# Two sets of edits to a hybrid mLSTM and expert-choice kernel: the barrier and the selection rounds between scan and experts; the order of first weights, small products and states

## The reference

```python
hn = rms_norm(x, norm1_g)
gb, gc, u, q, k, v, o, gates = split(hn @ w_in)          # 1024 x 3088
conv_out = gb * short_conv(gc * u, conv_w)
ht = mlstm_scan(q, k, v, li_f, lf_f) + flip(mlstm_scan(flip(q), ...))   # chunks of 128, both directions
mix = concat([conv_out, sigmoid(o) * head_norm(ht)])
x = x + mix @ w_out
tokens = rms_norm(x, norm2_g)
affinity = softmax(tokens @ w_router)                    # 16 experts
gate, idx = top_k(affinity.T, cap)                       # cap: 32 (prompt), 128 (sample)
ye = (silu(xe @ w_gate) * (xe @ w_up)) @ w_down * gate   # per expert, xe = tokens[idx]
y = rms_norm(x + scatter_add(ye, idx), final_g)
```

## Time and profile before

| what | us |
|---|---|
| median of 3 runs | 1314.3 |
| lowest and highest | 1312.56 and 1315.32 |
| profiled execution, its own time | 1317.02 |
| its span | 1315.3 |
| TensorE busy | 1259.4 |
| VectorE busy | 912.3 |
| ScalarE busy | 736.8 |
| GpSimd busy | 322.2 |

### The profile page before, as it was taken

The page is one execution under the profiler, slowest core; times in us unless marked ns, Lnnn a source line. Parts: engine busy times, 40 slices in busy tenths (PEclk is TensorE's granted clock), DMA queues, the critical chain, the costliest instruction groups (busy, mean ns, idle before and its releaser), DMA issues.

```text
span 1315.3 us, 25185 instructions
## 1 busy us (share of the span) xinstructions
PE 1259.4 (96%) x9826; PEld 1032.6 (79%) x9826; DVE 912.3 (69%) x1313; ACT 736.8 (56%) x1066; POOL 322.2 (25%) x316
## 2 busy tenths in 40 slices
PE   7999999999999999759999999999999999999993
PEld 6868987666587888659888988898889888988892
DVE  5463122442577555898889888988898889888975
ACT  6655322123334554346667666766676667666763
POOL 2511321010133331132232313131313131313040
PEclk8999999999999999979999999999999999999997
DMA  8131455251278774269999999999999999999895
GB/s 266 65 117 53 140 166 153 93 165 25 86 236 240 214 211 134 93 225 330 313 303 316 340 315 300 317 337 314 299 316 338 315 301 315 337 316 299 300 365 205
DMA packets 242032, 314.76 MB, mean 239 GB/s; under 512 B 16097, under 2 KB 206049, under 8 KB 241969
## 3 DMA queue, kind: packets, MB, share of 16 engines
q1 hardware_dynamic: 226576, 268.54, 62.1%
q0 software_dynamic: 15392, 45.36, 11.7%
HBM read 274.41 MB, written 39.44 MB: 239 GB/s over the span
## 4 chain that ended last, share of the span: by engine, by line
PE 89%; DVE 4%; ACT 2%; DMA 2%; issue 1%; SPq 0%; POOL 0%; DVEq 0%; ACTq 0%; POOLq 0%
PE psum L2182 22%; PE psum L2048 16%; PE psum L2189 11%; PE psum L2205 8%; PE psum L2030 8%; PE psum L1921 8%; PE psum L2223 4%; PE psum L2214 4%; PE psum L2175 1%; PE psum L1976 1%; DMA woraw<-in_w_out_dram 1%; ACT yt L1203 1%; PE psum L1902 1%; PE psum L1940 1%; PE psum L1981 1%
## 5 line engine op out<-in xcount | busy, mean ns | idle before, releaser
L1769 DVE TENSOR_TENSOR elo<-eraw,ehi 128x2048 bf16<-128x2048 f32 x192 | 433.4, 2284 | 1.0 <-POOLq L815 1.0
L1173 ACT ACTIVATE ehi<-eraw 128x2048 fp32r<-128x2048 f32 x192 | 362.3, 1903 | 26.5 <-PE psum L2223 18.6
L2182 PE MATMUL psum<-xc,ehi 128*128 128x320 f32 x2048 | 330.3, 313 | 2.1 <-DVE xc L1774 2.1
L2182 PEld LDWEIGHTS psum<-xc,ehi 128*128 128x128 f32 x2048 | 302.3, 188 | 3.6 <-DVE xc L1774 2.4
L2189 PE MATMUL psum<-xb,elo 128*128 128x160 bf16 x2048 | 163.9, 233 | 0.0
L1782 DVE TENSOR_REDUCE gu<-psum 128x320 f32<-128x640 f32 x128 | 105.2, 822 | 82.6 <-PE psum L2189 82.3
L2189 PEld LDWEIGHTS psum<-xb,elo 128*128 128x128 bf16 x2048 | 138.5, 98 | 13.1
L2048 PE MATMUL psum<-hn_nar,wnar 128*128 128x512 bf16 (+1 forms) x768 | 144.0, 344 | 0.0
L2205 PE MATMUL psum<-ehi,hc 128*128 128x512 f32 x512 | 132.6, 406 | 0.0
L2048 PEld LDWEIGHTS psum<-hn_nar,wnar 128*128 128x128 bf16 x768 | 72.9, 98 | 63.6 <-issue 4.9
L2205 PEld LDWEIGHTS psum<-ehi,hc 128*128 128x128 f32 x512 | 95.1, 188 | 22.2
(11 more groups left out here) (275 smaller groups left out, 1656.0 us busy)
## 6 DMA issues: line engine op xcount, KB each, us to landing
eraw<-in_w_gate_dram SPq DMA_DIRECT2D x64, 1024.0 KB, 8.9
eraw<-in_w_up_dram SPq DMA_DIRECT2D x64, 1024.0 KB, 8.8
eraw<-in_w_down_dram SPq DMA_DIRECT2D x64, 1024.0 KB, 13.0
wraw<-in_w_in_dram SPq DMA_DIRECT2D x12, 1024.0 KB, 7.5
negm<-negm_d SPq DMA_DIRECT2D x10, 512.0 KB, 6.5
acc_d<-x POOLq DMA_DIRECT2D x10, 512.0 KB, 5.4
tok_d<-tk POOLq DMA_DIRECT2D x10, 512.0 KB, 3.0
v<-v_d SPq DMA_DIRECT2D x18, 256.0 KB, 4.1
```

The costliest lines, as they stand in the source:

```text
L1173: act.activation(f["ehi"][:, j % RING, :], f["eraw"][:, raw_slot(s, j), :], ACT.Copy).then_inc(S["ehi"], 1)
L1769: dve.tensor_tensor(f["elo"][:, j % RING, :], f["eraw"][:, raw_slot(s, j), :], f["ehi"][:, j % RING, :].bitcast(F32), ALU.subtract).then_i ...
L2182: pe.matmul(o[:, 0:2 * NC], hi[:, k, c], x[:, k, :, :].rearrange("p a t -> p (a t)"), start=(k == 0), stop=False, skip_group_check=True)
```

## The change

The first set of edits: at the barrier GpSimd increments the semaphore without a drain. The index search of a round no longer waits for itself before the replacement (`ch.later`). The eight affinity tiles are transposed in two steps, seven right after the logits of tile 7 and the eighth two projection steps later; ScalarE copies the first seven, VectorE the eighth. The rounds are laid anew: 3, 2, 6, 1 and 4 in place of 1, 3, 2, 1, 1, 4 and 4. For the half residuals (8, 1), (9, 0) and (9, 1) TensorE adds x by a product with the identity and ScalarE copies the sum out (`residual_out`). `last_roots` polishes a root of ScalarE. ScalarE copies the prompt's rows to `AFF` and makes the prompt's part of the lists (`prompt_list`). The 48 unused transposes are 30, and VectorE makes two low weight splits instead of three ahead of expert 0's tokens.

The second set: SP waits for the weights of chunk 0 before it issues x tiles 2 to 9. VectorE splits the first half of these weights before it takes the low part of tile 0. The low products of tiles 0 and 1 go by operand (`low_first_tiles`). `router_weights` stands ahead of `out_low(4)` and no longer behind tile 1's heads. KEYS_AT and STATE_AT lie one group later.

```diff
+    def later(self, ins):
+        ins.then_inc(self.sem, 1)
+        self.n += 1
...
-    KEYS_AT = [of_chunk[4][7] + 3 * i for i in range(NT - 1)]
+    KEYS_AT = [of_chunk[4][8] + 3 * i for i in range(NT - 1)]
...
             load_chunk(0)
+            sp.wait_ge(w_ind[0], 16)
             for i in range(1, len(BATCHES)):
...
-            barrier(pool, 1)
+            pool.sem_inc(S["bar"], 1)
+            pool.wait_ge(S["bar"], 5)
...
+            def residual_out(m, h):
+
+                act.wait_ge(S["x1_done"], 2 * m + h)
+                act.wait_ge(S["o_ps"], 2 * m + h + 1)
+                if h == 0:
+                    act.wait_ge(x1_out[m % 2], 16 * (m // 2))
+                    act.wait_ge(S["sum2"], m - 1)
+                    act.wait_ge(S["tk_scaled"], 1)
+                act.activation(d["x1"][:, m % 2, 512 * h:512 * h + 512], psum[:, 6 + h, :], ACT.Copy
+                               ).then_inc(S["x1_done"], 1)
...
+                if n == NT + 1:
+                    act.wait_ge(S["sum2"], NT)
+                    act.activation(d["ms"][:, :, 1, H:H + 1], d["ms"][:, :, 0, H:H + 1], ACT.Sqrt,
+                                   bias=b["eps1"][:, 0:1]).then_inc(S["rooted"], 1)
+                    columns_out(n - 2, 1)
...
+                if n == NT:
+                    act.activation(spare_col, b["eps1"][:, 0:1], ACT.Sqrt)
+                    residual_out(n - 1, 0)
...
+                if n == NT - 1:
+
+                    act.wait_ge(S["choiceT_ps"], NS - 1)
+                    for i, w in ((0, half_width), (1, half_width - P)):
+                        act.activation(AFF[HALF2 * i:HALF2 * i + NE, 0:w], psum[0:NE, (0, 4)[i], 0:w], ACT.Copy
+                                       ).then_inc(S["aff_out"], 1)
...
+            act.wait_ge(S["choiceT_ps"], NS + 1)
+            act.activation(AFF[PROMPT:SEL, 0:SP_], psum[0:NE, 1, 0:SP_], ACT.Copy).then_inc(S["aff_out"], 1)
             arrive(act)
+
+            def prompt_list():
+
+                act.wait_ge(S["topk"], 1)
+                first, gates = GI[PROMPT:SEL, CAPS - CAPP:CAPS], GV[PROMPT:SEL, CAPS - CAPP:CAPS]
+                for j in range(4):
+                    i = act.activation(GIF[PROMPT:SEL, CAPP * j:CAPP * (j + 1)], first, ACT.Copy, scale=4.0,
+                                       bias=float(j))
...
+            split_low(0, 0, 4)
             tokens_low(0)
-            split_low(0, 0, 4)
...
-                    ch(dve.max_index(GI[rows, 8 * r:8 * r + 8], best, AFF[rows, 0:width]))
+                    ch.later(dve.max_index(GI[rows, 8 * r:8 * r + 8], best, AFF[rows, 0:width]))
...
+                ch(dve.tensor_scalar(d["ms"][:, :, 2, 0:1], d["ms"][:, :, 0, H:H + 1], EPS, None, ALU.add))
+                dve.wait_ge(S["rooted"], len(BATCHES) + 1)
+                polish(d["ms"][:, :, 1, H:H + 1], d["ms"][:, :, 2, 0:1], d["ms"][:, :, 2, H:H + 1])
...
+            router_weights()
             out_low(4)
...
+                    residual(n - 1, 0)
                     dve.wait_ge(S["aff_out"], NS // 4)
-                    choose(both_halves, half, CAPS, 0, 1)
...
+                    dve.wait_ge(S["choiceT_ps"], NS)
+                    last = slice(half - P, half)
+                    ch(dve.tensor_copy(AFF[HALF2:HALF2 + NE, last], psum[0:NE, 4, last]))
+                    choose(both_halves, half, CAPS, 0, 3)
...
+                    choose(both_halves, half, CAPS, 5, 11)
                     last_roots()
...
+                    choose(both_halves, half, CAPS, 11, 12)
...
-            dve.wait_ge(S["choiceT_ps"], 2)
-            ch(dve.tensor_copy(AFF[PROMPT:SEL, 0:SP_], psum[0:NE, 1, 0:SP_]))
+            dve.wait_ge(S["aff_out"], NS // 4 + 1)
             choose(slice(0, SEL), half, CAPS, 12, CAPS // 8)
...
-            for j in range(3):
+            for j in range(2):
                 low(0, 0, j)
...
+                    if with_x:
+                        pe.wait_ge(ld_x[n % 2], 16 * (n // 2 + 1))
+                        mm = pe.matmul(psum[:, 6 + h, :], ident[:, :], d["xs"][:, n % 2, c], start=False, stop=True)
...
+            def low_first_tiles():
+
+                pe.wait_ge(S["w_nar"], 1)
+                for g, of_x, of_w in ((0, LOW, HIGH), (0, HIGH, LOW), (1, HIGH, LOW), (1, LOW, HIGH)):
+                    if of_x == LOW:
+                        pe.wait_ge(S["hn_lo"], g + 1)
+                    else:
+                        pe.wait_ge(S["hn_nar"], g + 1)
+                        pe.wait_ge(S["w_lo"], 1)
...
+                if n == NT - 1:
+
+                    pe.wait_ge(S["aff_done"], NS - 1)
+                    pe.wait_ge(S["ht_done"], NT)
+                    for i in range(NS - 1):
+                        transpose_affinities(i).then_inc(S["choiceT_ps"], 1)
...
-            for _ in range(48):
+            for _ in range(30):
```

More of the change, by code:

```diff
@@ L1204, in final_sums @@
                                    accum_out=fs[:, 0, k:k + 1]).then_inc(S["f_sum"], 1)
-            for j in range(5):
+            for j in range(4):
                 high(0, 0, 0, j, True)
+            prompt_list()
+            high(0, 0, 0, 4, True)
             for g in range(3):
@@ L1801, in _ @@
                 tokens_low(0, 0, g, FIRST_BANKS[g])
-            for j in range(3, 5):
+            for j in range(2, 5):
                 low(0, 0, j)
```

86 lines of the change are left out of this document (42 added, 44 removed).

## The result

The changed kernel takes 1305.97 us (median of 4 runs, 1305.37 to 1308.95), the kernel before 1314.14 beside it (1312.56 to 1315.32). By the medians it is 8.2 us faster, where 18.6 were forecast; the time lies 1 us above the range given, 1291 to 1305. The ratio is 0.9947, with a 95% interval of 0.9935 to 0.9959, which stands for 5.4 to 8.5 us. Both profiled executions lie some 3 us over the median of their kernel, so their totals can be set against each other; where in the kernel the 3 us lie differs (see e8 and e14).

A forecast was written before the change was run, and what follows sets the result against it. TensorE, busy 96% of the span, was taken as the bound. Start 4.5, keys 2.1, router 3.3 and rounds with handover 8.7 summed to 18.6 us: median 1314.3 to 1295.7, given as 1296.5, range 1291 to 1305.

The forecast's parts named there:

- Start: First tiles: low products from 15.4 us, done at 20.1, next tile near 23.0 instead of 27.56; gain 4.5 us.
- The whole of 25.57: Start's upper bound: 5.4 us if the low products' end moves fully from 25.57 to 20.1.
- Keys: Keys and states one group later: wait near 176 us and slow clock behind it go; net gain 2.1 us.
- the wait before chunk sums 8: New TensorE wait at chunk 8 for weighed keys, caused by the later keys: 1.4 us, 1.6 more if the clock falls.
- Router: Router weights moved into VectorE's idle time before out_low(4): 1.65 us of wait and 1.7 of clock, together 3.3 us.
- Rounds: First round to last index, VectorE's work: earlier affinities, shorter root, fewer waits; 571.4 against 578.7, gain 7.3 us.
- Handover: Last index to expert 0's first products: 0.65 us from the list's last steps, 0.7 from the gather's end.
- 0.65 for the list: Handover: the list's last steps lose 0.25 and 0.43 us by moving to idle ScalarE.
- of which I take off 0.5 because loads 4 and 5 now overlap the gather: Handover: 1.2 us gained around the gather and its conversion, cut to 0.7 for 2 MB of overlapping loads.
- the handover eats the rounds: Rival, 0.07: token stores and loads 4 and 5 hold the gather; 7.3 us bring 2.0; gain 13.3, 1301.0.
- Costs nothing: GpSimd's drain at the barrier: covered before, and late stores end by 571.8, ahead of the list at 573.2.
- The rival of the clock: Rival, 0.25: clock falls at new gaps (start 1.6, chunk sums 8 1.6, expert 0 1); gain 14.4, 1299.9.

The follow-up runs named there:

- e8: Changed kernel with the old start (x loads not held back, low weights split later, low products tile by tile): 1308.26 us, ratio 0.9960.
- e14: Kernel before with one more GpSimd drain, ahead of its last two scatters: 1309.04 us, ratio 0.9961.
- e1: Changed kernel with the second set undone (start, keys and router as before): 1311.21 us, ratio 0.9983.
- e13: Changed kernel with router_weights() back at tile 1: 1308.15 us, ratio 0.9955.
- e2: Kernel before with the second set alone (start, keys, router): 1308.19 us, ratio 0.9952.
- e3: Changed kernel with expert 0's loads 4 and 5 held until the gather of its low halves has landed: 1309.33 us, ratio 0.9965.
- e6: Changed kernel with list ahead of fourth weight conversion, loads 4 and 5 held for the gather, fifth conversion behind token copies: 1301.39 us, ratio 0.9904.
- e11: Changed kernel with GpSimd's drain back at the barrier: 1305.66 us, ratio 0.9943.
- e4: Changed kernel with the prompt's list ahead of the fourth conversion of expert weights on ScalarE: 1304.87 us, ratio 0.9934.
- e10: e9 with 46 instead of 30 unused transposes and 15 more behind the gathered tokens' transposes, keeping TensorE busy: 1292.57 us, ratio 0.9844.
- e5: Changed kernel with one GpSimd drain added in idle time ahead of its last two scatters: 1299.12 us, ratio 0.9886.
- e9: Changed kernel with the edits of e5 and e6 together: 1293.46 us, ratio 0.9853.
- e7: Changed kernel with the wait between index search and replacement back in all rounds: 1305.80 us, ratio 0.9940.
- e12: Changed kernel with keys and states of chunk 4 one product group earlier, as before: 1307.50 us, ratio 0.9952.

## Why the prediction was wrong in its size

The direction was right and most mechanisms were. The step that failed is the handover, in two places that the prediction costed at nothing or less: the gather beside loads 4 and 5, and GpSimd's drain. Two terms of the second set were sized from a slow clock that belonged to one execution.

**Start, 4.5 us: 2.3 by the median (e8), 1.2 by the markers where the clock stays up.** The low products of the first tiles came as forecast but for 0.6 us (16.02, not 15.4, and done at 20.5, not 20.1). "The whole of 25.57" was wrong: 2.7 us of it were a clock of 0.57 in that one execution. The weights landed 0.1 us earlier, not 1.0 (10.56 for 10.70), and the x loads held back for that were not hidden: ScalarE waits 0.49 us for one. And the next tile started at 23.3 as said (23.0), but its low part, behind ScalarE and then VectorE, brought the gain down to 1.2.

**Keys, 2.1: right** (2.1 by the markers, 1.5 by the median), with the wait before chunk sums 8 at 1.19 us where 1.4 were forecast, and the clock not falling there.

**Router, 3.3: 2.2.** The wait is gone (0.29 us is left before L2002), which carried 1.6; the 1.7 for the clock were too much. e1, e13 and e14 have the old router and a clock of 1.00 from 397 to 407 us.

**Rounds, 7.3: 8.2.** Against the logits ahead of them the last index comes 15.9 - 7.7 = 8.2 us earlier. The first round is 5.87 us after the logits of tile 7 as forecast, the rounds save 2.0 us where 1.2 were taken.

**Handover, a gain of 1.35 forecast: a loss of 5.7** (26.7 against 21.0 from the last index to the third group), or of 4 beside the same handover in e2 and e14, whose first group ran at a lower clock (4.11 and 3.95 us) where the kernel before had 2.58. In place of "0.65 for the list", the list's product came 3.5 us after the last index, not 2.6: it is queued behind the fourth conversion, whose load had been safely ahead of the list when the list came 16 us later. In place of "of which I take off 0.5 because loads 4 and 5 now overlap the gather", the gather took 7.5 us to TensorE, against 4.2 alone (e3, e6), and TensorE, idle for 5.3 us, ran 16 products in 4.60 us instead of 2.58. The prediction had exactly this as its rival "the handover eats the rounds", with the right two transfers, at 0.07 and 2.0 us left of VectorE's 7.3; by the markers 8.2 - 5.7 = 2.5 were left. e6, which only unties these queues, brings the stretch back to 21.4 us and gains 4.6. That settles this part. One thing in it has no run of its own: the change also cut the unused transposes ahead of expert 0 from 48 to 30. e2 and e14 still have 48 and ran the first group in 4.11 and 3.95 us, so the cut is not all of the 2.0 us.

**GpSimd's drain, costed at 0: 2.26 us in the tail.** "Costs nothing" looked at the barrier alone, and there it was covered before. With the list earlier it would have held the list for 9 us (e11), at little cost, since the gather then had the queues to itself. Taken out, it made the drain that ends the program longer: 5.44 became 7.70, the same in every profiled kernel without the drain at the barrier and without the late one. No view of TensorE's waits shows that; the row stands among the sequencer's, behind the last product.

**Sum.** By the medians: second set 5.8, first set 2.8, together 8.2 instead of 18.6. By the traces the first set has 8.2 (rounds) less 4.1 (handover against e2, the kernel with the old one and the new start) less 2.3 (last drain) = 1.8; by the medians, the changed kernel against e2, 2.2. The low bounds of the prediction's terms added up to a gain of 8.4 us and to 1306, while its range stopped at 1305; the 8.2 measured are next to that sum, so the range was narrower than the prediction's own terms. What remains open is how often either start meets the slow clock: sixteen profiled executions, of sixteen kernels, are too few for that, and the median's 2.3 us lie between the 1.2 without it and the 3.8 to 4.1 by which e2 and e4 are ahead of the kernel before, which had it.

**The rival of the clock** had the right fact in the third of its places: it stood at 0.50 at expert 0, with a price of 2.0 us on the first products. Keeping TensorE busy there (e10) gave back 0.9 at most, as VectorE was next. The sums at 268 us kept their clock. The Trainium skill, "TensorE: Matmul & The Clock Gate", section "HAM oscillation", says that work behind a wait for a transfer starts cold. The three waits that the prediction names for it stood behind work of VectorE, not behind a transfer, and the clock was down after each. The traces agree as a tendency: the first group of expert 0 took 3.9 to 4.6 us in thirteen of sixteen kernels, eleven of which had waited for the gather (for 0.29 to 5.5 us), and 2.6 in the one where TensorE was kept busy (e10), but also in the kernel before and e11 behind waits of 2.1 us; at the start the same wait of 3.25 us left the clock down in two executions of four.

## What to carry to other kernels

When a change makes one stage earlier, write down every queue at the point where the next stage begins (ScalarE's conversions, the loads in flight, the gather) and ask which of them was ready only because the stage was late; here three such covers went at once (the list 0.9 us later behind a late load, the tokens 2.2 us later on TensorE from a gather beside other loads, 2.0 us of the clock), and untying the queues was worth more than half of the whole change. A slow clock in one profile can be a draw: the kernel before and e14 share their code there and differ by 4.2 us. Before a term takes its recovery in full, look for the same stretch in a second execution. And look behind the last product: a drain where GpSimd was idle cost nothing and took 4.9 and 6.9 us off two kernels, more than any of the terms forecast for the second set gave.

## What the hardware showed that I had not expected

GpSimd's drain is shorter when another drain has gone before it, even where nothing is under way: in the changed kernel the last one begins at 1299.3 us, after the last scatter has landed at 1299.12. As the first drain it took 9.06 us at the barrier (before, e2, e11, e14), 8.20 ahead of the last scatters (e5, e9, e10) and 7.70 at the end. Behind one at the barrier it took 5.87 ahead of the last scatters (e14) and 5.44 at the end (before, e2, e11), and behind a late one 0.21 to 0.22 at the end. Each of these times repeats to 0.01 us. The time since the drain before is not the measure (5.87 us after 707 us, but 5.44 after 739), they don't add up (8.20 and 0.22 are more than 7.70), and what the engine works through, the runs don't tell.

The second transfer of expert 0's gather takes 3.8 to 3.9 us from issue to landing by itself (before, e2, e3, e6, e9, e10, e11, e14) and 6.1 to 6.9 beside 2 MB of weights (changed, e1, e4, e5, e7, e8, e12, e13). Holding those weights until it has landed cost nothing in e6, where nothing that the experts waited for was queued behind them, and 3.4 us in e3, where the token copies were.
